# First block's compression: the blocks held stationary, both weight halves streamed in one matmul, the rows folded by a constant, and the logits behind map 0's scores

## The chip, the cores and the metric

The kernel runs on one core of one Trainium2 chip. What counts is the device time of the whole program, in microseconds (us), as the median of some runs. Three runs of the kernel before took 1732.04, 1733.45 and 1734.22 us. All arithmetic is in float32 (weights and activations of the large products are held as two fp32r parts).

## What is computed

A program of four layers on one sequence of 256 tokens with 1024 channels: two layers of the "first block" and two of the "second block". The change touches the first block alone, and in it the attention over compressed keys and values. Cut to that:

```python
def compress(t, pos_emb, w1, b1, w2):            # t: 256 tokens, 2 groups, 64 channels
    # 15 overlapping blocks of 32 tokens each, stride 16
    flat = blocks(t + pos_emb).reshape(15, 2, 32 * 64)
    hid = gelu(flat @ w1 + b1)                   # w1: 2048 x 128
    return hid @ w2                              # w2: 128 x 64
...
kc = compress(kcb, ..., cmp_w1[0], ...)          # n = 0 in the kernel: keys
vc = compress(vcb, ..., cmp_w1[1], ...)          # n = 1: values
s_c = einsum(q_raw, kc) * scale                  # 8 heads, 256 queries, 15 blocks
p_c = masked_softmax(s_c, ...)
o_b = gate0 * (p_c @ vc) + gate1 * (selected attention) + gate2 * (window attention)
```

## The kernel before

**Weights.** Every weight arrives in chunks of 1 MB in the ring `raw` (3 slots), issued by SyncE (`load`; the load of chunk c waits until chunk c - 3 is split). ScalarE rounds a chunk to its high part `whi` (two halves, L543), VectorE subtracts to get the low part `wlo` (L893); both have rings of 4 slots. `split_to(c)` does this, and where it stands in the queues of ScalarE and VectorE is written out by hand, mostly three chunks ahead of the products. A slot comes free when the sums that read it are done.

**Tiles.** `tile` makes 128 output channels for 256 tokens: for each of 8 pieces k of the contraction one matmul with `whi` as stationary operand and 512 columns (activations high | low, L1457) and one with `wlo` and 256 columns (L1460). Columns 0 to 255 and 256 to 511 of the bank are two parts of the sum: ScalarE copies the second to `low` (`low_copy`), VectorE adds the first (`tile_sum`, L901) and signals `tile_out`. Tile t uses bank t % 4, with exceptions in `EXTRA` and `PLACED`, and waits for the sum of tile t - 4.

**A layer of the first block.** Eight chunks of `w_in`, with rotary products between them; then the gate chunks `early 0` to `early 3`, each of two tiles. Beside the 16 steps of `early 0` run those of `compress(0)`, beside `early 1` those of `compress(1)`: after each pair of tile matmuls one with `whi` stationary and 60 columns (15 blocks x 2 groups, high | low, `RH`, L1608), one with `wlo` and 30 columns (L1609). The chunks are numbered through: `early 0` is chunk 8 of layer 0, the first compression chunk 9, `early 1` 10, the second compression chunk 11, `early 2` and `early 3` 12 and 13, then come the chunks of the branches, 14 and on. ScalarE and VectorE pass the same order as steps c of a loop; c = 9 and 11 are the compression's. There the 30 columns are summed into `HC`, and GELU is applied.

Then come, on TensorE: tile `early 2,0` (the first of the pair), a wait for both halves of `HC`, the second-stage products (L1678, L1680), tile `early 2,1`, a wait for ScalarE's copy to `KC` and `VC`, the logits (16 products of 64 rows, L1690), a wait for the sum of `early 2,1`, and the attention loop over 18 maps. Its steps i = 0 and 1 hold the scores of maps 0 and 1 (L1715), each followed by a tile of `early 3`; in steps 2 and 3 the compressed probabilities `PC` are transposed (L1726) and copied by ScalarE to `PCT` (shown as U). On VectorE the logits' mask, maximum and subtraction (L1107 to L1116) stand ahead of map 0; the sum of `early 2,1` stands behind the split of chunk 15 (`split_to(p["early"][3][0] + 2)`), on ScalarE too. Layer 1 is the same code.

## Time and profile before

| | |
|---|---|
| median of three runs | 1733.45 us |
| the profiled execution | 1734.53 us |
| its span, first to last instruction | 1732.7 us |
| granted TensorE clock, mean of the span | 0.998 of 2.4 GHz |
| TensorE busy (matmuls / weight loads) | 1705.6 us, 98% / 1455.9 us, 84% |
| VectorE, ScalarE, GpSimd busy | 1221.0 us, 70%; 1022.4 us, 59%; 690.5 us, 40% |
| compression products L1608, L1609 | 64 each, of 9926 matmuls in all |
| chain of work that ended last, by engine | PE 76%, DVE 17%, ACT 3% |

The busy share of TensorE counts a matmul from start to modelled end, and they overlap; how fast the queue moves is read from the starts of successive matmuls. PE is TensorE's matmuls, PEld its weight loads, DVE VectorE, ACT ScalarE, POOL GpSimd, SP SyncE.

### The profile page before, as it was taken

To read this page: it belongs to the slowest core of one execution; us is meant where nothing else is said; L and a number is where in the kernel's file an instruction comes from. 1 tells how busy PE (TensorE), PEld (TensorE's weight loads), DVE (VectorE), ACT (ScalarE), POOL (GpSimd) and SP (SyncE) were. 2 spreads that over 40 slices of the span, in tenths; PEclk is the share of its full clock that TensorE was granted. 3 is DMA by queue.
4 is the path that set the end of the run, shared out by engine and by line. 5 is a ranking of instruction groups with operands and counts; after the bars stand their busy time and mean duration, and the time that the engine had idled before them with its cause. 6 is when DMAs were issued, how large, how long until landed. Compare 5 with 4: busy or idle time off the path is not lost.

```text
span 1732.7 us, 26430 instructions
## 1 busy us (share of the span) xinstructions
PE 1705.6 (98%) x9926; PEld 1455.9 (84%) x9926; DVE 1221.0 (70%) x1840; ACT 1022.4 (59%) x1928; POOL 690.5 (40%) x666
## 2 busy tenths in 40 slices
PE   8999999999999999999999999999999999999998
PEld 7867898888867898889888888888898889788887
DVE  7776799957766799957666656766476656566663
ACT  5577666655577666646555556555465545565542
POOL 4135256701035256604661050765057600507640
PEclk9999999999999999999999999999999999999999
DMA  9633576576524576576766553866576565348662
GB/s 271 175 98 109 171 208 182 174 244 175 146 77 122 170 201 189 182 231 173 193 183 223 176 172 98 234 184 206 178 201 188 183 231 193 123 124 224 187 208 73
DMA packets 412226, 306.73 MB, mean 177 GB/s; under 512 B 10083, under 2 KB 366901, under 8 KB 412098
## 3 DMA queue, kind: packets, MB, share of 16 engines
q1 hardware_dynamic: 411314, 304.31, 59.8%
q8 instruction: 79, 1.29, 0.3%
q0 software_dynamic: 784, 0.72, 0.2%
q14 instruction: 49, 0.40, 0.1%
HBM read 303.94 MB, written 1.05 MB: 176 GB/s over the span
## 4 chain that ended last, share of the span: by engine, by line
PE 76%; DVE 17%; ACT 3%; issue 3%; DMA 1%; DVEq 0%; SPq 0%; ACTq 0%
PE bank L1457 26%; PE bank L1460 13%; PE bank L1557 8%; PE bank L1559 8%; PE bank L1558 8%; DVE wlo L893 6%; DVE CB L1221 6%; PE bank L1523 3%; PE bank L1520 3%; DVE UB L901 2%; PE bank L1491 1%; PE bank L1764 1%; ACT PB L546 1%; PE bank L1739 1%; PE bank L1715 1%
## 5 line engine op out<-in xcount | busy, mean ns | idle before, releaser
L893 DVE TENSOR_TENSOR wlo<-raw,whi 128x1024 fp32r<-128x1024 f32 (+1 forms) x568 | 735.9, 1319 | 174.2 <-ACT whi L543 170.6
L1457 PE MATMUL bank<-hsA,whi 128*128 128x512 f32 x2480 | 797.5, 398 | 0.0
L543 ACT ACTIVATE whi<-raw 128x1024 fp32r<-128x1024 f32 (+1 forms) x568 | 571.4, 1034 | 133.9 <-PE bank L1559 89.1
L1460 PEld LDWEIGHTS bank<-hsA,wlo 128*128 128x128 f32 x2480 | 467.1, 188 | 105.8
L1460 PE MATMUL bank<-hsA,wlo 128*128 128x256 f32 x2480 | 495.6, 279 | 0.0
L1457 PEld LDWEIGHTS bank<-hsA,whi 128*128 128x128 f32 x2480 | 384.6, 189 | 3.0 <-issue 2.2
L543 ACT ACTIVATE low<-bank 128x256 f32<-128x256 f32 (+1 forms) x404 | 150.3, 376 | 315.8 <-PE bank L1457 289.0
L1325 POOL TENSOR_TENSOR HB<-CB,UB 128x256 f32<-128x256 f32 x88 | 123.6, 1405 | 343.3 <-ACT CB L546 342.7
L1557 PE MATMUL bank<-whi,hid 128*128 128x512 f32 x528 | 206.1, 390 | 2.0 <-DVE wlo L893 2.0
L1559 PE MATMUL bank<-wlo,hid 128*128 128x512 f32 x528 | 205.5, 389 | 0.0
L1558 PE MATMUL bank<-whi,hid 128*128 128x512 f32 x528 | 205.4, 389 | 0.0
L901 DVE TENSOR_TENSOR UB<-bank,low 128x256 f32<-128x256 f32 x264 | 109.2, 416 | 113.0 <-ACT low L543 112.8
L1326 POOL TENSOR_TENSOR hid<-CB,UB 128x256 fp32r<-128x256 f32 x88 | 144.9, 1646 | 0.0
L1557 PEld LDWEIGHTS bank<-whi,hid 128*128 128x128 f32 x528 | 99.1, 188 | 23.0 <-DVE wlo L893 2.8
L1325 POOL TENSOR_TENSOR HB<-CB 128x256 f32<-128x256 f32 x44 | 62.0, 1408 | 139.5 <-ACT CB L546 139.5
L1559 PEld LDWEIGHTS bank<-wlo,hid 128*128 128x128 f32 x528 | 99.1, 188 | 20.6
L1558 PEld LDWEIGHTS bank<-whi,hid 128*128 128x128 f32 x528 | 99.1, 188 | 20.5
L1221 DVE SCALAR_TENSOR_TENSOR CB<-UB,convT,CB 128x256 f32<-128x256 f32 x176 | 114.0, 705 | 0.0
L1327 POOL TENSOR_TENSOR hid<-HB,hid 128x256 fp32r<-128x256 f32 x132 | 109.7, 831 | 10.4
L1523 PE MATMUL bank<-hsA,wlo 128*128 128x256 f32 x464 | 96.5, 284 | 0.0
L1520 PE MATMUL bank<-hsA,whi 128*128 128x256 f32 x464 | 94.2, 283 | 0.0
L1523 PEld LDWEIGHTS bank<-hsA,wlo 128*128 128x128 f32 x464 | 78.8, 192 | 0.7
(226 smaller groups left out, 1896.1 us busy)
## 6 DMA issues: line engine op xcount, KB each, us to landing
raw<-in_ffn_w_up SPq DMA_DIRECT2D x176, 512.0 KB, 5.3
raw<-in_ffn_w_down SPq DMA_DIRECT2D x120, 512.0 KB, 4.5
raw<-in_w_in SPq DMA_DIRECT2D x104, 512.0 KB, 5.9
raw<-in_ffn_w_gate SPq DMA_DIRECT2D x88, 512.0 KB, 4.1
raw<-in_w_out SPq DMA_DIRECT2D x32, 512.0 KB, 4.5
raw<-in_ffn_w_down SPq DMA_DIRECT2D x24, 256.0 KB, 2.9
G<-in_norm_g SPq DMA_DIRECT2D x12, 512.0 KB, 7.2
raw<-in_cmp_w SPq DMA_DIRECT2D x8, 512.0 KB, 5.4
```

What stands on the lines that cost most here:

```text
L543: return nc.scalar.activation(out_, in_, func, **kw)
L893: v.tensor_tensor(wlo[c_ % RING][:, x:y], raw[:, c_ % RAW, x:y], whi[c_ % RING][:, x:y].bitcast(F32), ALU.subtract)\
L1221: ins = v.scalar_tensor_tensor(y[:, n, :], UB[:, j % 2, n, k:S + k], convT[:, k, at:at + 1], y[:, n, :], ALU.mult, ALU.add)
L1325: g_.tensor_tensor(HB[:, j % 2, :], x, y, ALU.mult)
L1326: seq.link(g_.tensor_tensor(dst[:, 0:S], x, y, ALU.mult))
L1457: return mm(out_[:, 0:2 * n], whi[slot][:, at:at + P], rhs[:, 0:2 * n], start=x == 0, stop=False, **g32)
L1460: return mm(out_[:, n:2 * n], wlo[slot][:, at:at + P], rhs[:, 0:n], start=False, stop=False, **g32)
L1520: return mm(out_, whi[c % RING][:, at(m, k):at(m, k) + P], both(k, 1), start=False, stop=j == 0 and k == KD - 1, **g32)
L1523: return mm(tile_bank(t + m)[:, S:2 * S], wlo[c % RING][:, at(m, k):at(m, k) + P], hsA[:, k, 0:S], start=False, stop=j > 0 and k == KD - 1 ...
L1557: mm(y, hi, whi[s][:, x * HALF:x * HALF + HALF], start=k == k_first, stop=False, **g32)
L1558: mm(y, lo, whi[s][:, x * HALF:x * HALF + HALF], start=False, stop=False, **g32)
L1559: ins = mm(y, hi, wlo[s][:, x * HALF:x * HALF + HALF], start=False, stop=k == k_end, **g32)
```

## The change

- The compression's product is turned round. Stationary is now a window of 128 columns of the blocks (`RHP`: the 60 columns of step k, the 60 of step k + 1 and 8 more; behind the last step 68 columns of zeros), moving are 128 columns of `whi` and the same 128 of `wlo`, in one matmul of 256 columns. For that both lie in one tensor `whl`. The result has blocks in its rows (0 to 59 count) and hidden units in its columns.
- ScalarE copies the 60 x 128 of the second half, VectorE adds the first into `HE`. A new product per n, `fold`, multiplies `HE` with a constant 128 x 30 matrix: it adds rows i and i + 30 and transposes, into bank 7 or 6. GELU reads that bank. `fold(0)` stands behind the first tile of `early 1`, `fold(1)` behind `early 2,0`.
- `HE` and the zeros are filled by GpSimd at the start of each layer's rotation products, `KC` (now zero-padded by parity of the head) once by VectorE at the start.
- The second-stage products stand behind `early 2,1`. The logits are 8 products of 128 rows against the padded `KC`, 30 columns each, and stand behind the scores of map 0 on TensorE; on VectorE their part stands behind map 0, on ScalarE their exponential behind map 0's.
- The splits at c = 9 and 11 move behind the compression's copy and sum; the split of chunk 15 moves behind the sum of `early 2,1` on both engines, and on VectorE its second half behind the logits.

```diff
...
-    whi = [sb(f"whi{n}", [P, CH], F32R)[0] for n in range(RING)]
-    wlo = [sb(f"wlo{n}", [P, CH], F32R)[0] for n in range(RING)]
+    whl = sb("whl", [P, RING, 2, CH], F32R)[0]
+    whi, wlo = [[whl[:, n, x, :] for n in range(RING)] for x in range(2)]
...
+    HE = sb("HE", [P, 2, P], at=hsB_at + 4096)[0]
+    RHP, _, rh_end = sb("RHP", [P, 2, 16 * 4 * N_CMP + 68], F32R, at=hsB_at + 8128)
...
@@ scalar, steps c
-                if not early:
+                if not early and c not in (9, 11):
                     split_to(in_cs[c] + 3)
...
                 if c in (9, 11):
-                    low_copy(p["cmp"][c // 2 - 4][1], n=30)
+                    t = p["cmp"][c // 2 - 4][1]
+                    act.wait_ge(sum_ready, t + 1)
+                    f(low[0:4 * N_CMP, t % 4, 0:P], tile_bank(t)[0:4 * N_CMP, P:2 * P], ACT.Copy).then_inc(low_ready, 1)
...
                 if c in (9, 11):
+                    split_to(in_cs[c] + 3)
                     n = c // 2 - 4
-                    act.wait_ge(tile_out, p["cmp"][n][1] + 1)
-                    f(HC[:, n, :], HC[:, n, :], ACT.Gelu_apprx_tanh,
+                    act.wait_ge(cmp_fold, 2 * L + n + 1)
+                    f(HC[:, n, :], bank[7 - n][:, S:S + 2 * N_CMP], ACT.Gelu_apprx_tanh,
...
             low_copy(third)
+            low_copy(third + 1)
             act.wait_ge(cmp_kv, L + 1)
...
-            f(KC[:, :], bank[6][:, 0:30], ACT.Copy)
+            for e in range(2):
+                r = slice(HD * e, HD * e + HD)
+                f(KC[r, :, N_CMP * e:N_CMP * e + N_CMP], bank[6][r, 0:30].rearrange("p (g c) -> p g c", g=2), ACT.Copy)
             f(VC[0:N_CMP, :, :], ...).then_inc(cmp_kv_out, 1)
             split_to(p["early"][3][0] + 2)
-            low_copy(third + 1)
-            act.wait_ge(cmp_x, L + 1)
-            f(PC[:, :, :, 0:N_CMP], PC[:, :, :, 0:N_CMP], ACT.Exp, scale=SCALE).then_inc(cmp_e, 1)
...
+                if i == 0:
+                    act.wait_ge(cmp_x, L + 1)
+                    f(PC[:, :, :, 0:N_CMP], PC[:, :, :, 0:N_CMP], ACT.Exp, scale=SCALE).then_inc(cmp_e, 1)
@@ vector
-                    tile_sum(p["cmp"][c // 2 - 4][1], HC[:, c // 2 - 4, :], n=30)
+                    n, t = c // 2 - 4, p["cmp"][c // 2 - 4][1]
+                    dve.wait_ge(low_ready, t + 1)
+                    dve.wait_ge(cmp_clear, 2 * L + 2)
+                    r = slice(0, 4 * N_CMP)
+                    v.tensor_tensor(HE[r, n, :], tile_bank(t)[r, 0:P], low[r, t % 4, 0:P], ALU.add).then_inc(tile_out, 1)
+                    split_to(in_cs[c] + 3)
...
             tile_sum(third, gate_place(2)[:, 0, :])
-            split_to(p["early"][3][0] + 2)
             tile_sum(third + 1, gate_place(2)[:, 1, :])
+            split_to(p["early"][3][0] + 2, 0)
...
+                if i == 0:
+                    cmp_scores()
+                    split_to(p["early"][3][0] + 2)
@@ gpsimd
+            pool.wait_ge(ht_ready, h_at(2 * L, 1, 1))
+            g_.memset(HE[:, :, :], 0.0).then_inc(cmp_clear, 1)
+            g_.memset(RHP[:, :, 16 * 4 * N_CMP:].bitcast(F32), 0.0).then_inc(cmp_clear, 1)
@@ tensor
-                        mm(out_[:, 0:60], whi[slot][:, k * P:k * P + P], RH[:, n, k, :], start=k == 0, stop=False, **g32)
-                        ins = mm(out_[:, 30:60], wlo[slot][:, k * P:k * P + P], RH[:, n, k, 0:30], start=False, stop=k == 15, **g32)
+                        at = k * 4 * N_CMP
+                        ins = mm(out_[:, 0:2 * P].rearrange("p (x j) -> p x j", x=2), RHP[:, n, at:at + P],
+                                 whl[:, slot, :, k * P:k * P + P], start=k == 0, stop=k == 15, **g32)
...
+            def fold(n):
+                pe.wait_ge(tile_out, p["cmp"][n][1] + 1)
+                if n == 0:
+                    pe.wait_ge(swap_used, 11 * L + len(ROPE))
+                mm(bank[7 - n][:, S:S + 2 * N_CMP], HE[:, n, :], C("fold"), start=True, stop=True, **g32).then_inc(cmp_fold, 1)
...
             for m in range(2):
                 early_tile(1, m, compress(1)(m))
+                if m == 0:
+                    fold(0)
             early_tile(2, 0)
+            fold(1)
+            early_tile(2, 1)
             pe.wait_ge(cmp_hid, 2 * L + 2)
...
             ins.then_inc(cmp_kv, 1)
-            early_tile(2, 1)
-            pe.wait_ge(cmp_kv_out, L + 1)
...
+            def cmp_scores():
+                pe.wait_ge(cmp_kv_out, L + 1)
+                for qb in range(2):
+                    for j in range(4):
+                        at = (4 * qb + j) * 32
+                        ins = mm(bank[7][:, at:at + 2 * N_CMP], U1[:, QB + j, qb * P:qb * P + P], KC[:, j // 2, :],
+                                 start=True, stop=True, **g32)
+                ins.then_inc(cmp_z, 1)
...
-            pe.wait_ge(tile_out, third + 2)
+            pe.wait_ge(tile_out, max(t for t in range(third + 2) if t % 4 < 2) + 1)
...
                     if i == 1:
-                        pe.wait_ge(cmp_x, L + 1)
+                        pe.wait_ge(gates_ready, L + 1)
...
+                if i == 0:
+                    cmp_scores()
+                    pe.wait_ge(tile_out, third + 2)
```

## Rows read from the trace of the kernel before

**Rows 1.** TensorE's timeline, plain tiles: start us, us, engine, line, operation, count

```profile
62.13 0.63 PE L1457 MATMUL bank<-hsA,whi 128*128 128x512 f32 x2
...
62.83 0.62 PE L1457 MATMUL bank<-hsA,whi 128*128 128x512 f32 x2
```

**Rows 2.** TensorE's timeline beside the compression, layer 0, first to last of eight steps

```profile
74.35 0.19 PE L1608 MATMUL bank<-RH,whi 128*128 128x60 f32 x1
74.38 0.26 PE L1609 MATMUL bank<-RH,wlo 128*128 128x30 f32 x1
74.49 0.48 PE L1457 MATMUL bank<-hsA,whi 128*128 128x512 f32 x1
...
79.08 0.48 PE L1457 MATMUL bank<-hsA,whi 128*128 128x512 f32 x1
```

**Rows 3.** TensorE's timeline, first and last of 27 starts, 256 columns

```profile
24.84 0.28 PE L1520 MATMUL bank<-hsA,whi 128*128 128x256 f32 x1
...
27.96 0.28 PE L1520 MATMUL bank<-hsA,whi 128*128 128x256 f32 x1
```

**Rows 4.** TensorE's timeline, layer 0, second stage to transposes; [idle before <-releaser]

```profile
94.39 0.41 PE L1678 MATMUL bank<-HC,w2cur 128*128 128x30 f32 x2 [1.25 <-ACT HC L546]
...
95.05 0.50 PE L1457 MATMUL bank<-hsA,whi 128*128 128x512 f32 x1
...
98.04 1.96 PE L1690 MATMUL bank<-KC,U 64*128 64x15 f32 x32
...
100.47 0.50 PE L1457 MATMUL bank<-hsA,whi 128*128 128x512 f32 x1
...
107.74 1.05 PE L1726 MATMUL bank<-const,PC 128*15 128x128 f32 x8
```

**Rows 5.** VectorE's timeline, layer 0

```profile
90.26 0.75 DVE L901 TENSOR_TENSOR SGE<-bank,low 128x256 f32<-128x256 f32 x2
...
96.48 2.36 DVE L893 TENSOR_TENSOR wlo<-raw,whi 128x1024 fp32r<-128x1024 f32 x2 [1.42 <-ACT whi L543]
...
100.12 0.60 DVE L1107 TENSOR_TENSOR PC<-bank,const 128x60 f32<-128x60 f32 x4 [0.94 <-PE bank L1690]
...
101.73 0.35 DVE L1146 CUSTOM_DVE_ANT_0 PB<-bank,const,nsink 128x128 f32<-128x128 f32 x1
...
104.48 0.48 DVE L1146 CUSTOM_DVE_ANT_0 PB<-bank,const,nsink 128x256 f32<-128x256 f32 x1
```

**Rows 6.** ScalarE's timeline, layer 0

```profile
95.25 0.25 ACT L543 ACTIVATE VC<-bank 15x128 f32<-15x128 f32 x1
95.40 1.99 ACT L543 ACTIVATE whi<-raw 128x1024 fp32r<-128x1024 f32 x2
...
106.60 0.19 ACT L546 ACTIVATION_READ_ACCUMULATOR PB<-PB,st 128x1 f32 x1
...
108.39 1.06 ACT L543 ACTIVATE U<-bank 15x512 f32<-15x512 f32 x2 [0.79 <-PE bank L1726]
```

**Rows 7.** Chain of waits, layer 0: start us, us, what

```profile
28.61 0.86 PE bank L1657 x4
...
121.42 0.66 PE bank L1764 x8
```

**Rows 8.** Page, costliest groups: busy us, mean ns, idle before and releaser

```profile
L543 ACT ACTIVATE low<-bank 128x256 f32<-128x256 f32 (+1 forms) x404 | 150.3, 376 | 315.8 <-PE bank L1457 289.0
```

**Rows 9.** TensorE's timeline, layer 1

```profile
479.33 0.50 PE L1457 MATMUL bank<-hsA,whi 128*128 128x512 f32 x1
...
485.47 0.34 PE L1715 MATMUL bank<-U 64*128 64x128 f32 x1 [1.18 <-DVE SGE L901]
```

**Rows 10.** ScalarE's timeline, layer 1

```profile
495.56 1.06 ACT L543 ACTIVATE U<-bank 15x512 f32<-15x512 f32 x2 [0.79 <-PE bank L1726]
```

**Rows 11.** Chain of waits, layer 1

```profile
471.27 10.24 DMA raw<-in_w_in
```

**Rows 12.** Stretches, layer 1: busy us (count) of each engine, granted clock, DMA, GB/s

```profile
486.00:488.00 2.00, 2.00 (x10) 1.60 (x7) 1.93 (x11) 0.40 (x1) 0.00 (x0) 0.55 0.95 287
```

More of the change, by code:

```diff
@@ L43 @@
 CONST = {"ident": 128, "swap": 128, "ntri": 128, "stick": 128, "mask_a": 256, "mask_c": 256, "pair": 24,
-         "mask_cmp": 32, "count": 32, "width": 2, "freq": 1, "sign": 1}
+         "mask_cmp": 32, "count": 32, "width": 2, "freq": 1, "sign": 1, "fold": 2 * N_CMP}
 CONST_AT, _n = {}, 0
@@ L76, in host_constants @@
     put("sign", np.where(i % 64 < 32, -1.0, 1.0))
+    put("fold", (i[:, None] < 4 * N_CMP) & (i[:, None] % (2 * N_CMP) == np.arange(2 * N_CMP)[None, :]))
     return c
@@ L212, in build @@
     stc = sb("stc", [P, 4, 16])[0]
-    KC = sb("KC", [P, 30])[0]
+    KC = sb("KC", [P, 2, 2 * N_CMP])[0]
     VC = sb("VC", [16, 2, HD], at=cq_at)[0]
@@ L984, in _ @@
         v.memset(col[:, 1:2], 1.0)
+        v.memset(KC[:, :, :], 0.0)
         def turns():
@@ L1068, in _ @@
                 early = L == 0 and c < 4
-                if not early:
+                if not early and c not in (9, 11):
                     split_to(in_cs[c] + 3)
@@ L1113, in per_row @@
                 return stc[:, k, :].unsqueeze(2).broadcast_to([P, 16, N_CMP])
-            seq.link(v.tensor_reduce(stc[:, 0, :], rowsP, AX_X, ALU.max))
-            seq.link(v.tensor_scalar(stc[:, 0, :], stc[:, 0, :], 0.1 * NEG, None, ALU.max))
-            v.tensor_tensor(rowsP, rowsP, per_row(0), ALU.subtract).then_inc(cmp_x, 1)
+            def cmp_scores():
+                dve.wait_ge(gates_ready, L + 1)
+                dve.wait_ge(cmp_z, L + 1)
+                z = bank[7][:, 0:S].rearrange("p (b h c) -> p b h c", b=2, h=4)
+                mask = C("mask_cmp").rearrange("p (b c) -> p b c", b=2)
+                for qb in range(2):
+                    for par in range(2):
+                        ins = v.tensor_tensor(PC[:, qb, par:8:2, 0:N_CMP], z[:, qb, :, N_CMP * par:N_CMP * par + N_CMP],
+                                              mask[:, qb:qb + 1, 0:N_CMP].broadcast_to([P, 4, N_CMP]), ALU.add)
+                seq.link(ins)
+                seq.link(v.tensor_reduce(stc[:, 0, :], rowsP, AX_X, ALU.max))
+                seq.link(v.tensor_scalar(stc[:, 0, :], stc[:, 0, :], 0.1 * NEG, None, ALU.max))
+                v.tensor_tensor(rowsP, rowsP, per_row(0), ALU.subtract).then_inc(cmp_x, 1)
             gate = gates[:, :, :].rearrange("p b (h n) -> p (b h) n", n=3)
@@ L1682, in _, with cmp_scores @@
             ins.then_inc(cmp_kv, 1)
-            early_tile(2, 1)
-            pe.wait_ge(cmp_kv_out, L + 1)
-            pe.wait_ge(rope_done, 11 * L + len(ROPE))
-            for qb in range(2):
-                for h in range(8):
-                    r, at = HD * (h % 2), (4 * qb + h // 2) * 16
-                    ins = mm(bank[7 - 2 * (h % 2)][:, at:at + N_CMP], U1[r:r + HD, QB + h // 2, qb * P:qb * P + P],
-                             KC[r:r + HD, N_CMP * (h // 4):N_CMP * (h // 4) + N_CMP], start=True, stop=True, **g32)
-            ins.then_inc(cmp_z, 1)
-            third, fourth = p["early"][2][1], p["early"][3][1]
+            third, fourth = p["early"][2][1], p["early"][3][1]
+            def cmp_scores():
+                pe.wait_ge(cmp_kv_out, L + 1)
+                for qb in range(2):
+                    for j in range(4):
[3 more added lines that the diff above has]
+                ins.then_inc(cmp_z, 1)
+            pe.wait_ge(rope_done, 11 * L + len(ROPE))
             pe.wait_ge(kswap_done, 3 * L + 3)
-            pe.wait_ge(tile_out, third + 2)
+            pe.wait_ge(tile_out, max(t for t in range(third + 2) if t % 4 < 2) + 1)
             done = len(MAPS) * L
```

16 lines of the change are left out of this document (5 added, 11 removed).

## The prediction

> **What bounds the kernel now.** I read the page first: TensorE is busy 98% of the span (the table above), so time goes only where TensorE's queue gets shorter or where it stands still. Then TensorE's timeline in the stretch that the diff touches, once in each layer of the first block (about 71 to 108 us, and 455 to 496 us), then ScalarE and VectorE in the same stretch, and last the chain of waits behind it. Times of the first layer (layer 0) are in us from the span's start.
>
> Ahead of the stretch and behind it nothing is edited but small fills. What has to be found is by how much the attention loop is entered earlier in each layer. Everything behind is bounded by TensorE and its weights are prefetched only three chunks deep, so I take the shift as kept to the end of the program.
>
> **Compression products.** Two plain matmul pairs of a tile (512 and 256 columns each) repeat every 0.70 us, 0.35 a pair [rows 1]. With the compression beside them eight steps take 79.08 - 74.49 = 4.59 us, 0.575 a step [rows 2]. The 60-column and the 30-column matmul thus cost 0.225 us a step, though their columns are few: the 30-column one starts 0.03 us after the other, and the next tile matmul another 0.11 later [rows 2]. That is the pace of 128-column weight loads which nothing covers. The change puts one load and one 256-column matmul in the place of two and two. 256 columns cost 0.12 us where moving data comes in two pieces of 128 at stride, as it will here: 27.96 - 24.84 = 3.12 us from the first to the last of 27 starts, the load hidden [rows 3]. New step 0.35 + 0.12 = 0.47, saved 0.105. Bounds: 0.117 (the column pace of the plain tile, 0.35 x 256/768) and 0.23 (load exposed, 0.11 more). There are 32 steps in a layer: **-3.4 us** (bounds -3.5 and +0.2).
>
> By the Trainium skill (TensorE: Matmul & The Clock Gate, LDWEIGHTS and Back-to-back issue gap) a load takes as long as its number of columns, 128/1.2 = 107 ns, and 256 columns stream in 109 ns; an estimate from these would hide the load by 2 ns and give a step of 0.46, 0.3 us more saved in a layer. The rule also speaks against the change, since 60 of the 128 columns of a window would do: padded, the load has no slack left. The rows agree on the 0.11.
>
> **Folding.** Two new f32 products a layer, 128 columns stationary, 30 moving. The nearest rows are the f32 products of the second stage, which come as two instructions of 30 and four of 64 columns between 94.39 and 95.05, 0.11 each [rows 4]: 0.22 to 0.33 each fold, 0.3 taken, **+0.6 us**. The fold waits for VectorE's sum of the 60 rows. For `fold(1)` (layer 0): TensorE ends `early 2,0` at 94.39 - 1.25 = 93.1 today [rows 4], 3.4 - 0.3 earlier then, 90.0. VectorE begins the two sums of `early 1` at 90.26, right behind its split of chunk 13, and they take 0.75 [rows 5]; that split moves by 1.7 (below), so the sums end at 89.3 and `HE`, priced at 0.2, at 89.5. No wait, with 0.5 us in hand.
>
> **The hidden layer's wait.** Today TensorE stands still 1.25 us until GELU is done [rows 4], because the second-stage product sits in the middle of tile pair `early 2`. Moved behind the pair it has 2.8 us of cover (eight pairs): **-1.25 us**.
>
> **Logits.** 16 products of 64 rows become 8 of 128 rows. Every f32 product is two instructions; 32 of 64 rows now run in pairs, one on each half of the array, 1.96 us for the 32 [rows 4], so 0.11 a pair, and 16 full-height ones at 0.11 take the same 1.8 us. **0**; less instructions buy nothing (bounds -0.9 if each took half a pair, +0.1). The Trainium skill (TensorEngine Tiling, Theoretical Speedup) gives two row tiles up to twofold and so says that the change throws that away; the row agrees, and it is just as much as the halved count gives back. The gap before the logits, 98.04 - (95.05 + 2.8) = 0.2 us, goes, since map 0's scores now stand before them: `KC` is copied in two halves, one copy (0.1 us) more before `cmp_kv_out`.
>
> TensorE in layer 0: second stage done at 95.05 - 3.4 + 0.6 - 1.25 + 2.8 (tile 2,1 now ahead) = 93.8. Logits and map 0's scores take 98.04 to 100.47 today, 2.43 [rows 4]; done at 96.2. Tile `early 3,0` started at 100.47: **-4.3 us** there, and the transposes of the probabilities, today 107.74, at 103.45.
>
> **What is late next.** The chain runs on through ScalarE: from its copy of the transposed probabilities at 108.39 [rows 6] it is the chain's main engine until TensorE takes over at 121.4 [rows 7]. So the entry is that copy, and it has a second way of being late. VectorE and ScalarE in the new order: `cmp_kv_out` follows the second stage by 95.50 - 95.05 = 0.45 us, plus 0.1 [rows 4, 6]: 94.35. Then ScalarE splits the first half of chunk 15 (half of 1.99) to 95.35, VectorE its half (half of 2.36) to 96.5 [rows 5, 6], and both stand ahead of map 0 in their queues. VectorE then has map 0 and the normalising (101.73 to 104.48, 2.75), the logits (100.12 to 101.73, 1.61) and the second half of the split (1.18), in all to 102.05; map 1 and its exponentials (104.48 to 106.79) 104.35 [rows 5, 6]; one copy of a tile half, 0.38 [rows 8]: **104.75**, against 104.05 by TensorE. 108.39 - 104.75 = **-3.65 us in layer 0**.
>
> Layer 1 runs the same code 384.3 us later, by one instruction in both, the first of tile `early 2,1` (95.05 and 479.33) [rows 4, 9]. Its entry is at 495.56 today, 111.26 in layer-0 time, 2.9 later than there [rows 6, 10]. The chain shows why: the load of chunk 15 was 10.24 us under way, to 481.51 [rows 11]; ScalarE's split waited for it, VectorE behind that, the tile sum behind that, and TensorE lost 1.18 us [rows 9]. Then its clock fell to 0.55 of full, the 1.2 GHz level for most of 486 to 488 [rows 12]. The change takes the sum out from behind the split. But it leaves map 0 and the logits behind the split's first half. That load is issued after the split of chunk 12, which moves with the first 16 steps, 1.7 us; landing at 479.8, 95.5 in layer-0 time, where ScalarE could start at 94.35. So everything of the chain is 1.15 us later than in layer 0: entry 105.9, and 111.26 - 105.9 = **-5.35 us in layer 1**. In layer 1 map 0 must also wait for the sum of `early 2,1` (banks 0 and 1), 0.4 us; the 2 us of slack that TensorE has there hide it.
>
> **Small things.** GpSimd fills `HE` and the tail of `RHP` before its first rotation product: nearest rows 0.1 to 0.3 us each, and TensorE, behind it, has no idle time in its timeline from 24 to 48 us; 0. VectorE's fill of `KC` at the start lies before its wait for ScalarE; 0. SyncE: loads 15 to 17 come 1.7 to 2 us earlier, load 18 about 2 us later, for a chunk used only behind the attention loop; 0. `RH` padding moves no bytes.
>
> **Sum.** -3.65 - 5.35 = -9.0 us. On the profiled execution 1734.5 - 9.0 = 1725.5; that execution is 1.1 us above the median, so the median becomes 1733.45 - 9.0 = **1724.4 us**.
>
> **The rivals.** (a) *Chunk 15 lands in time in layer 1*: its slow load may be an accident of what else is in flight, and in layer 0 the same load holds nobody up. Then layer 1 gains 6.5: **1723.3 us**. (b) *The load of the window is not hidden* (0.11 more a step): for it, that load and stream are within 0.01 us of each other. The second stage ends 3.4 us later again, entry 108.1 in both layers, -0.3 and -3.2: **1729.9 us**. (c) *The fold becomes the wait*: `HE` is summed behind a chunk split and two tile sums, in hand are 0.5 us. Beyond that it is paid in full in layer 0, and in layer 1 less the 1.15 us that chunk 15 hides. Late by 2.1 us, 1.6 beyond: 1.6 + 0.45 = 2.05, **1726.4 us**. (d) *Clock*: three microseconds of small products in a row (to 96.2) are new, and at the level of 1.2 GHz the tiles behind them would cost 1.5 us more; TensorE has 0.7 us in hand in layer 0 and 2 in layer 1, so 0.8 us: **1725.2**, within the forecast. The Trainium skill (TensorE: Matmul & The Clock Gate, HAM oscillation) has idle gaps as the cause; such a gap precedes the fall of [rows 9, 12], and the change removes it. (e) *The other side*: the 256-column matmul runs at the pace of unsplit f32, 0.86 us for four, twice over (0.43) [rows 7], if one operand is not taken as fp32r. That adds 0.31 a step, 19.8 us in all: **1744 us**. It decides from 0.26 us per matmul on. Against it: all three operands are declared fp32r.
>
> **How the numbers follow.** Forecast with (d) 0.62; (a) 0.14; (b) 0.08; (c) 0.10; (e) 0.04; other 0.02. Range: (a) with fold and step at their lower bounds, 1721.0; up to between (c) and (b), 1729.0. A difference of 0.2% (3.5 us) is about what a measurement of this kernel can tell from none: (b) lies on that line. Faster 0.88, same 0.07, slower 0.05.
>
> **What would show it.** Steps with compression at 0.47 us; fold 0.3 us with no idle before it; no idle before the second stage; logits still 1.8 us; tile `early 3,0` at 96.2; ScalarE's copy of the probabilities at 104.75 in layer 0 and at 495.56 - 9.0 = 486.6 in layer 1 (all there is shifted by layer 0's gain); the wait of ScalarE for chunk 15 still there in layer 1; the fall of the clock behind it gone. Wrong would be: a step of 0.58, or an attention loop that starts earlier but leaves ScalarE later than 121.4 - 3.65, or a shift that shrinks in a later stage.

## The result, and the profile after

| | before | after |
|---|---|---|
| median | 1733.84 us (1732.04 to 1734.43, 4 runs) | 1724.54 us (1723.51 to 1726.55, 4 runs) |
| the profiled execution | 1734.53 us | 1723.51 us |
| its span | 1732.7 us | 1721.7 us |
| granted TensorE clock, mean | 0.998 | 1.000 |
| matmuls | 9926 | 9838 |

The ratio is 0.995, 95% interval 0.9939 to 0.9962: 9.3 us less, where 9.0 had been forecast. Run again later in two more series, the changed kernel took 1724.29 and 1724.85 us.

The page of the changed kernel, busy times and share of the span; the shares are those of before within a point:

```profile
span 1721.7 us, 26269 instructions
PE 1697.1 (99%) x9838; PEld 1448.0 (84%) x9838; DVE 1220.8 (71%) x1841; ACT 1023.1 (59%) x1930; POOL 691.8 (40%) x670
```

Times of two executions can't be laid side by side as they stand: the first compression product is at 71.38 us before and at 70.72 us after, with nothing edited ahead of it but fills. So I count layer 0 from that product, layer 1 from layer 0's entry, and the rest from layer 1's entry. "Entry" is ScalarE's copy of the transposed probabilities, as in the prediction.

| | before | after | difference | forecast |
|---|---|---|---|---|
| first compression product | 71.38 | 70.72 | -0.66 | 0 |
| layer 0: to the entry | 37.01 | 32.94 | -4.07 | -3.65 |
| entry to entry | 387.17 | 380.89 | -6.28 | -5.35 |
| entry of layer 1 to the end of the span | 1237.1 | 1237.15 | 0 | 0 |

TensorE's timeline in layer 0 (columns as in [rows 1]; answers to [rows 2, 4]). L1482 and L1485 are the tile's two matmuls, L1635 the compression, L1647 the fold, L1716 and L1718 the second stage, L1754 map scores, L1729 the logits, L1768 the transposes:

```profile
79.29 0.39 PE L1482 MATMUL bank<-hsA,whl 128*128 128x512 f32 x1
79.52 0.28 PE L1635 MATMUL bank<-whl,RHP 128*128 128x256 f32 x1
...
80.22 0.39 PE L1482 MATMUL bank<-hsA,whl 128*128 128x512 f32 x1
...
82.10 0.39 PE L1482 MATMUL bank<-hsA,whl 128*128 128x512 f32 x1
...
82.44 0.30 PE L1647 MATMUL bank<-const,HE 128*128 128x30 f32 x2
82.58 0.48 PE L1482 MATMUL bank<-hsA,whl 128*128 128x512 f32 x1
...
83.25 0.39 PE L1482 MATMUL bank<-hsA,whl 128*128 128x512 f32 x1
...
88.98 0.40 PE L1482 MATMUL bank<-hsA,whl 128*128 128x512 f32 x1
89.21 0.30 PE L1647 MATMUL bank<-const,HE 128*128 128x30 f32 x2
89.35 0.47 PE L1482 MATMUL bank<-hsA,whl 128*128 128x512 f32 x1
...
92.23 0.30 PE L1716 MATMUL bank<-HC,w2cur 128*128 128x30 f32 x2
...
92.79 0.37 PE L1754 MATMUL bank<-U 64*128 64x128 f32 x1
...
93.62 1.97 PE L1729 MATMUL bank<-KC,U 128*128 128x30 f32 x16
95.43 0.48 PE L1482 MATMUL bank<-hsA,whl 128*128 128x512 f32 x1
...
102.67 1.05 PE L1768 MATMUL bank<-const,PC 128*15 128x128 f32 x8
```

What to see: two steps in 80.22 - 79.29 = 0.93 us; no idle time at either fold, and the two steps around the first take 83.25 - 82.10 = 1.15 us, 0.22 more than two steps elsewhere; no idle time before the second stage, where 1.25 us stood in [rows 4]; 1.81 us from the logits to the tile behind them, as before.

ScalarE's timeline in layer 0 (answers to [rows 6]) and VectorE's (answers to [rows 5]):

```profile
93.30 0.27 ACT L548 ACTIVATE VC<-bank 15x128 f32<-15x128 f32 x1
93.47 1.99 ACT L548 ACTIVATE whl<-raw 128x1024 fp32r<-128x1024 f32 x2
...
102.30 0.20 ACT L551 ACTIVATE st<-st 128x2 f32<-128x2 f32 x1 [2.90 <-DVE st L1170]
...
103.66 1.05 ACT L548 ACTIVATE U<-bank 15x512 f32<-15x512 f32 x2
```

```profile
88.53 0.27 DVE L1098 TENSOR_TENSOR HE<-bank,low 60x128 f32<-60x128 f32 x1
...
94.55 1.23 DVE L904 TENSOR_TENSOR whl<-raw,whl 128x1024 fp32r<-128x1024 f32 x1 [1.28 <-ACT whl L548]
...
98.58 1.22 DVE L904 TENSOR_TENSOR whl<-raw,whl 128x1024 fp32r<-128x1024 f32 x1
...
101.18 0.48 DVE L1165 CUSTOM_DVE_ANT_0 PB<-bank,const,nsink 128x256 f32<-128x256 f32 x1
```

The entry follows ScalarE's exponentials of map 1 without idle time, and these waited 2.90 us for VectorE: VectorE's queue, with both halves of the split in it, sets the entry, as forecast, not the transposes.

Layer 1, TensorE, ScalarE, chain of waits, and a stretch (busy us and count of PE, PEld, DVE, ACT, POOL, then granted clock, DMA share, GB/s), answering to [rows 9 to 12]:

```profile
472.46 0.30 PE L1716 MATMUL bank<-HC,w2cur 128*128 128x30 f32 x2
...
473.65 0.34 PE L1754 MATMUL bank<-U 64*128 64x128 f32 x1 [0.56 <-DVE SGE L912]
```

```profile
474.34 2.00 ACT L548 ACTIVATE whl<-raw 128x1024 fp32r<-128x1024 f32 x2 [0.54 <-DMA raw<-in_w_in]
...
484.55 1.05 ACT L548 ACTIVATE U<-bank 15x512 f32<-15x512 f32 x2
```

```profile
465.12 9.20 DMA raw<-in_w_in
```

```profile
476.00:478.00 2.00, 2.00 (x14) 1.78 (x14) 1.97 (x12) 1.66 (x3) 0.00 (x0) 1.00 1.19 295
```

The load of chunk 15 is still waited for, but only 0.54 us, and the clock is full, where [rows 12] had 0.55.

### The profile page after: what moved, and what is told of

It reads as the page before. It is cut to its first block, busy times and chain, and to the rows that moved or that the text cites. A ratio compares the mean times of both kernels' runs of the same rounds, so it can differ in the third digit from the quotient of the medians.

```text
span 1721.7 us, 26269 instructions
## 1 busy us (share of the span) xinstructions
PE 1697.1 (99%) x9838; PEld 1448.0 (84%) x9838; DVE 1220.8 (71%) x1841; ACT 1023.1 (59%) x1930; POOL 691.8 (40%) x670
## 4 chain that ended last, share of the span: by engine, by line
PE 75%; DVE 17%; ACT 3%; issue 3%; DMA 1%; DVEq 0%; SPq 0%; ACTq 0%
PE bank L1482 26%; PE bank L1485 13%; PE bank L1582 8%; PE bank L1583 8%; PE bank L1584 8%; DVE whl L904 6%; DVE CB L1243 6%; PE bank L1548 3%; PE bank L1545 3%; DVE UB L912 2%; PE bank L1516 1%; ACT PB L551 1%; PE bank L1806 1%; PE bank L1781 1%; DVE hsA L976 1%
## 5 line engine op out<-in xcount | busy, mean ns | idle before, releaser
L904 DVE TENSOR_TENSOR whl<-raw,whl 128x1024 fp32r<-128x1024 f32 (+1 forms) x568 | 735.5, 1318 | 169.4 <-ACT whl L548 165.8
L1482 PE MATMUL bank<-hsA,whl 128*128 128x512 f32 x2480 | 793.4, 397 | 0.0
L548 ACT ACTIVATE whl<-raw 128x1024 fp32r<-128x1024 f32 (+1 forms) x568 | 571.3, 1034 | 141.2 <-PE bank L1584 85.9
L1485 PEld LDWEIGHTS bank<-hsA,whl 128*128 128x128 f32 x2480 | 466.0, 188 | 105.5
L1485 PE MATMUL bank<-hsA,whl 128*128 128x256 f32 x2480 | 491.9, 278 | 0.0
L1482 PEld LDWEIGHTS bank<-hsA,whl 128*128 128x128 f32 x2480 | 384.0, 189 | 3.9 <-issue 2.4
L1582 PE MATMUL bank<-whl,hid 128*128 128x512 f32 x528 | 206.1, 390 | 2.0 <-DVE whl L904 2.0
L1584 PE MATMUL bank<-whl,hid 128*128 128x512 f32 x528 | 205.5, 389 | 0.0
L1583 PE MATMUL bank<-whl,hid 128*128 128x512 f32 x528 | 205.4, 389 | 0.0
L1582 PEld LDWEIGHTS bank<-whl,hid 128*128 128x128 f32 x528 | 99.1, 188 | 23.1 <-DVE whl L904 2.9
L1584 PEld LDWEIGHTS bank<-whl,hid 128*128 128x128 f32 x528 | 99.1, 188 | 20.7
L1583 PEld LDWEIGHTS bank<-whl,hid 128*128 128x128 f32 x528 | 99.1, 188 | 20.4
L1349 POOL TENSOR_TENSOR hid<-HB,hid 128x256 fp32r<-128x256 f32 x132 | 109.6, 831 | 10.3
L1548 PE MATMUL bank<-hsA,whl 128*128 128x256 f32 x464 | 96.4, 284 | 0.0
L1545 PE MATMUL bank<-hsA,whl 128*128 128x256 f32 x464 | 94.2, 283 | 0.0
L1548 PEld LDWEIGHTS bank<-hsA,whl 128*128 128x128 f32 x464 | 78.8, 191 | 0.7
```

The lines of the kernel that those rows point to most:

```text
L548: return nc.scalar.activation(out_, in_, func, **kw)
L904: v.tensor_tensor(wlo[c_ % RING][:, x:y], raw[:, c_ % RAW, x:y], whi[c_ % RING][:, x:y].bitcast(F32), ALU.subtract)\
L1482: return mm(out_[:, 0:2 * n], whi[slot][:, at:at + P], rhs[:, 0:2 * n], start=x == 0, stop=False, **g32)
L1485: return mm(out_[:, n:2 * n], wlo[slot][:, at:at + P], rhs[:, 0:n], start=False, stop=False, **g32)
L1545: return mm(out_, whi[c % RING][:, at(m, k):at(m, k) + P], both(k, 1), start=False, stop=j == 0 and k == KD - 1, **g32)
L1548: return mm(tile_bank(t + m)[:, S:2 * S], wlo[c % RING][:, at(m, k):at(m, k) + P], hsA[:, k, 0:S], start=False, stop=j > 0 and k == KD - 1 ...
```

## The experiments

All comparisons with the kernel before are between runs of one chip. Where an experiment's share of the gain is given for a layer, it is taken from its profiled execution with the three marks of the table above.

### One half alone: the turned product and the fold

The order of second stage, logits and splits of chunk 15 is that of before; the product, the fold, the padded `KC` and the moved splits at c = 9 and 11 stay.

```diff
@@ scalar
-            low_copy(third + 1)
@@ ... behind split_to(p["early"][3][0] + 2)
+            low_copy(third + 1)
+            act.wait_ge(cmp_x, L + 1)
+            f(PC[:, :, :, 0:N_CMP], PC[:, :, :, 0:N_CMP], ACT.Exp, scale=SCALE).then_inc(cmp_e, 1)
@@ vector: the split of 15 ahead of tile_sum(third + 1), cmp_scores() behind it
@@ tensor
             fold(1)
-            early_tile(2, 1)
             pe.wait_ge(cmp_hid, 2 * L + 2)
...
+            early_tile(2, 1)
...
+            cmp_scores()
```

> The changed kernel with the turned product and the folds kept, but the order of before for the rest: second stage in the middle of tile pair early 2 (behind fold(1)), logits ahead of map 0, sum of early 2,1 behind the split of chunk 15. Theory (TensorE's queue to the second stage, then the landing of chunk 15 in layer 1): 32 steps of 0.467 in place of 0.575, -3.5 us, folds at 0.14 each, +0.3; the wait for GELU about 0.5 us in place of 1.25. Layer 0 enters the attention loop 4.0 us earlier than before; in layer 1 the start of map 0 hangs on the landing of chunk 15, which moves by only 1.7 us, so only that is gained there and the stall of TensorE before map 0 grows from 1.2 to over 3 us, with the fall of the clock behind it. In all -5.7 us, 1728.1. Rival (the gain is simply a sum of TensorE's terms): -4.0 in both layers, 1725.8, stall unchanged.

Measured: 1728.57 us (1727.23 to 1729.81), ratio 0.9971 (0.996 to 0.9982). Layer 0 -3.91, entry to entry -2.53. TensorE's timeline in layer 0, then in layer 1, then two stretches of layer 1 in the columns used above:

```profile
90.03 0.41 PE L1712 MATMUL bank<-HC,w2cur 128*128 128x30 f32 x2 [0.38 <-ACT HC L551]
```

```profile
478.49 0.43 PE L1752 MATMUL bank<-U 64*128 64x128 f32 x1 [2.68 <-DVE SGE L911]
```

```profile
478.00:480.00 2.00, 1.51 (x9) 1.29 (x10) 1.90 (x10) 0.22 (x1) 0.00 (x0) 0.67 0.77 186
480.00:482.00 2.00, 2.00 (x8) 1.71 (x8) 1.90 (x13) 1.06 (x5) 0.00 (x0) 0.50 1.08 377
```

The wait for the hidden layer has fallen from 1.25 to 0.38 us with the old order: GELU now follows the fold directly, and VectorE sums ahead of its split. In layer 1 the opposite: the earlier the compression is done, the longer the sum of `early 2,1` waits behind chunk 15. ScalarE waits 2.83 us for the load, TensorE 2.68 us for the sum (1.18 in [rows 9]), and the clock falls to its lower level. The product saves 3.9 us in layer 0 and 2.5 in layer 1: some 1.4 us of it is taken back there, less than the 2.3 that had been expected.

### The other half alone: the order

The product of before (two matmuls a step, `whi` and `wlo` stationary), no fold; everything in the new order.

```diff
-                        ins = mm(out_[:, 0:2 * P].rearrange("p (x j) -> p x j", x=2), RHP[:, n, at:at + P],
-                                 whl[:, slot, :, k * P:k * P + P], start=k == 0, stop=k == 15, **g32)
+                        mm(out_[:, 0:60], whi[slot][:, k * P:k * P + P], RH[:, n, k, :], start=k == 0, stop=False, **g32)
+                        ins = mm(out_[:, 30:60], wlo[slot][:, k * P:k * P + P], RH[:, n, k, 0:30], start=False, stop=k == 15, **g32)
...
-                if m == 0:
-                    fold(0)
...
-            fold(1)
```

> The changed kernel with the product of before (two matmuls of 60 and 30 columns a step, the sum of 30 columns into HC, no fold), all else of the change kept. Theory: steps at 0.575 again; second stage without a wait. The entry of the attention loop (ScalarE's copy of the transposed probabilities) follows cmp_kv_out by the same 10.2 us as in the changed kernel: layer 0 about 1.1 us earlier than before (107.3). Layer 1: no stall ahead of map 0 but 0.5, no fall of the clock, entry 3.9 earlier than before in addition. In all -5.0 us, 1728.8. Rival (most of layer 1's gain comes from the shorter products): -1.1 in layer 0 and as much in layer 1, 1731.6, with stall and slow clock still there.

Measured: 1730.5 us (1729.11 to 1731.75), ratio 0.998 (0.9972 to 0.9989). Layer 0 -1.32, entry to entry -4.14. ScalarE doesn't wait for chunk 15 and the clock is 1.00 in layer 1 from 474 us on; TensorE waits for the sum of `early 2,1` as forecast, 0.56 us:

```profile
480.29 0.34 PE L1749 MATMUL bank<-U 64*128 64x128 f32 x1 [0.56 <-DVE SGE L912]
```

The two local gains, -1.32 - 4.14 = -5.46, lie within 0.5 us of what was expected; the median moved by 3.3 only (more on this in the part on the sum and the median). The halves together: -3.91 - 1.32 in layer 0 against -4.07 of the whole, since both take from the same wait for the hidden layer (0.87 of its 1.25 us goes by the first half alone) and the whole is held by VectorE; -2.53 - 4.14 = -6.67 against -6.28 from entry to entry.

### Only the sum ahead of the split, in the kernel before

```diff
@@ scalar
-            split_to(p["early"][3][0] + 2)
             low_copy(third + 1)
+            split_to(p["early"][3][0] + 2)
@@ vector
-            split_to(p["early"][3][0] + 2)
             tile_sum(third + 1, gate_place(2)[:, 1, :])
+            split_to(p["early"][3][0] + 2)
```

> The kernel before with one thing moved: copy and sum of tile early 2,1 ahead of the split of chunk 15, on ScalarE and VectorE. Theory: layer 0 unchanged. In layer 1 TensorE's wait of 1.18 us ahead of map 0 and the slow clock behind it (1.5 us) go; the logits' mask and maximum on VectorE are still behind the split, 0.3 us of the loss stays. -2.5 us, 1731.3. Rival (the chain through the split is the limit, the sum's place does not matter): the entry stays at 495.6, 1733.8; or the clock falls all the same: -1.2, 1732.6.

Measured: 1731.88 us (1731.12 to 1733.3), ratio 0.9992 (0.9983 to 1.0001). Layer 0 +0.18, entry to entry 384.45, which is -2.72. No stall of TensorE for that sum and a clock of 1.00 throughout layer 1. Before, layer 1's entry lay 387.17 - 384.3 = 2.9 us further behind layer 0's than the same instruction's distance [rows 4, 9] would have it; this edit of four lines takes 2.7 of them. So in the traced execution the late entry of layer 1 was that sum behind chunk 15, and the clock behind it. The median moved by 1.9 us with an interval that touches no change.

### The kernel before, once more

> The kernel before once more, for its profile. Theory: the late landing of chunk 15 in layer 1, TensorE's wait of over 1 us ahead of map 0 and the slow clock behind it are there in every execution; distance from the entry of layer 0 to that of layer 1 387.2 us as in the first profile. Rival: they differ from execution to execution (distance between 384.3 and 387.2), and the median contains only part of them.

Measured: 1734.15 us. The stall and the clock return, by TensorE's timeline, ScalarE's, the chain and a stretch:

```profile
485.01 0.34 PE L1715 MATMUL bank<-U 64*128 64x128 f32 x1 [1.09 <-DVE SGE L901]
```

```profile
481.08 2.00 ACT L543 ACTIVATE whi<-raw 128x1024 fp32r<-128x1024 f32 x2 [1.66 <-DMA raw<-in_w_in]
```

```profile
470.90 10.16 DMA raw<-in_w_in
```

```profile
486.00:488.00 2.00, 2.00 (x8) 1.71 (x8) 1.93 (x12) 0.63 (x3) 0.00 (x0) 0.50 0.99 347
```

Entry to entry is 387.03 here and 387.17 there: neither stall nor fall is an accident of the first trace. That every execution has them does not follow from two traces, and the clocks of the others speak against it (see the part on the sum and the median).

### The changed kernel, twice more

> The changed kernel once more, timed beside the others on the same chip. Both theories: 1724.5 us, 9.3 below before; the entry of the attention loop 4.1 us earlier in layer 0 once the start of the program is taken off, ScalarE's wait for chunk 15 in layer 1 between 0 and 2 us.

Measured: 1724.29 us (1723.47 to 1726.03), ratio 0.9946 (0.9934 to 0.9958). Layer 0's entry is at 32.93, entry to entry takes 381.02, the wait for chunk 15 is 0.65 us, and the clock doesn't fall in either layer.

> The changed kernel itself, on the same chip as the 64-row logits. 1724.4 us by both theories; clock 1.00 in 96 to 102 us by theory A, by theory B it may as well fall here.

Measured: 1724.85 us (1724.13 to 1726.66), ratio 0.9952 (0.9935 to 0.9969). Here the two distances are 32.93 and 380.95, the wait is 0.58 us, and the clock is 1.00 in both layers. The distances repeat to 0.15 us in three executions; what varies is the place of the first compression product, 70.72, 71.56 and 71.91 us, ahead of all that was changed.

### Sixty columns of the window for 128

```diff
-                        ins = mm(out_[:, 0:2 * P].rearrange("p (x j) -> p x j", x=2), RHP[:, n, at:at + P],
+                        ins = mm(out_[0:4 * N_CMP, 0:2 * P].rearrange("p (x j) -> p x j", x=2), RHP[:, n, at:at + 4 * N_CMP],
```

> The changed kernel with the window cut to the 60 columns that count: 60 stationary columns in place of 128, result in rows 0 to 59 alone. Theory (in the changed kernel the load is hidden and the step is bound by its 1024 streamed columns): step stays 0.467 us, no change, 1724.4. Rival (the load of 128 columns is the last to end, the rule that a load takes as long as its columns): up to 0.01 us a step, 0.6 us in all, hardly to be seen; or a narrow load is slower, as the 15-column loads in the trace do not show: then the step grows above 0.5 and the time above 1726.

Measured: 1724.65 us (1723.34 to 1725.62), ratio 0.9944 (0.9932 to 0.9956). The next start is 0.12 us behind the product as before (72.87 to 72.99 in its timeline):

```profile
72.87 0.28 PE L1635 MATMUL bank<-whl,RHP 128*60 128x256 f32 x1
72.99 0.40 PE L1482 MATMUL bank<-hsA,whl 128*128 128x512 f32 x1
```

So the 128-column load is hidden behind the 256 columns, and rival (b) is out. In this execution the clock fell to 0.50 in layer 1 from 478 to 480 us, and entry to entry took 0.8 us more than in the changed kernel. Ahead of the fall stand the wait for the sum of `early 2,1`, 0.56 us as in the changed kernel, and the logits in their 128-row form. It was one execution; whether the narrower window has a part in it is open.

### The logits as 16 products of 64 rows

```diff
-                    for j in range(4):
-                        at = (4 * qb + j) * 32
-                        ins = mm(bank[7][:, at:at + 2 * N_CMP], U1[:, QB + j, qb * P:qb * P + P], KC[:, j // 2, :],
+                    for h in range(8):
+                        r, at = HD * (h % 2), (4 * qb + h // 2) * 32
+                        ins = mm(bank[7 - h % 2][:, at:at + N_CMP], U1[r:r + HD, QB + h // 2, qb * P:qb * P + P],
+                                 KC[r:r + HD, h // 4, N_CMP * (h % 2):N_CMP * (h % 2) + N_CMP], start=True, stop=True, **g32)
```

> The changed kernel with the logits as 16 products of 64 rows again, into two banks, in their new place. Theory (pairs of 64-row instructions run side by side, so halving their count bought nothing): the 32 instructions take 1.8 us as the 16 do; no change, 1724.4. Rival (each instruction has its own price of 0.11 us): 3.6 us, and since VectorE's chain hangs on them, up to 1.8 us more in a layer, 1728.

Measured: 1725.42 us (1725.05 to 1725.94), ratio 0.9948 (0.9935 to 0.996). The product itself is as short as forecast, 1.89 us to the next tile against 1.81. But layer 0's entry came 34.18 us behind the first compression product, not 32.94. TensorE's timeline and three stretches of layer 0:

```profile
94.51 1.86 PEld L1729 LDWEIGHTS bank<-KC,U 64*128 64x128 f32 x32 [0.31 <-ACT VC L548]
94.51 1.96 PE L1729 MATMUL bank<-KC,U 64*128 64x15 f32 x32
96.40 0.50 PE L1482 MATMUL bank<-hsA,whl 128*128 128x512 f32 x1
...
97.69 1.06 PE L1482 MATMUL bank<-hsA,whl 128*128 128x512 f32 x2
```

```profile
96.00:98.00 2.00, 2.00 (x18) 1.84 (x17) 1.97 (x12) 1.66 (x3) 0.00 (x0) 0.91 1.07 276
98.00:100.00 2.00, 2.00 (x7) 1.62 (x7) 1.90 (x8) 2.00 (x10) 0.00 (x0) 0.50 0.10 31
100.00:102.00 2.00, 2.00 (x11) 1.19 (x10) 1.86 (x6) 0.40 (x2) 0.00 (x0) 0.74 0.05 14
```

The clock is at its lower level (0.50 of full, 1.2 GHz) from 97.6 to 101.0 us by the shares of these stretches, and two tile matmuls take 1.06 us instead of 0.63. TensorE had waited 0.31 us for `VC` ahead of the logits, and not otherwise; from the last start of map 0's scores to the first of the logits it is 0.39 us here and 0.40 in the changed kernel, so this wait doesn't tell the two apart. In layer 1 ScalarE waited 1.19 us for chunk 15 in this execution, and entry to entry took 381.58 us. This was a result that no theory had named, so the kernel was run again beside the changed one:

> The changed kernel with the logits as 16 products of 64 rows again, run once more. In its first execution TensorE's granted clock fell to 0.50 in layer 0 behind the logits, where it had been 1.00 in both executions of the changed kernel, and the entry of the attention loop came 1.2 us later. Theory A: the lower clock belongs to the 64-row form standing behind map 0's scores, which are 64-row products too; then it is below 1.00 in layer 0 (96 to 102 us) again and the median is 1 us above that of the changed kernel run beside it (about 1725.4 against 1724.4). Theory B: it was an accident of one execution; then the clock is 1.00 there, layer 0's entry is 32.9 us behind the first compression product as in the changed kernel, and the medians agree within 0.5 us.

Measured: 1725.51 us (1723.59 to 1726.5), ratio 0.9952 (0.9937 to 0.9966). Its stretches in layer 0:

```profile
96.00:98.00 2.00, 2.00 (x10) 1.79 (x9) 1.97 (x14) 1.67 (x4) 0.00 (x0) 0.70 0.68 197
98.00:100.00 2.00, 2.00 (x8) 1.63 (x7) 1.90 (x5) 1.61 (x9) 0.00 (x0) 0.50 0.00 1
```

The fall repeats, with the entry at 34.24 us. In the three traced executions of the changed kernel the clock is 1.00 in these stretches and the entry at 32.93 or 32.94, and the four other traces with 128-row logits in this place (the order alone, sixty columns, chunk 15 twice) have no fall in layer 0 either. So theory A holds for the place and the cost, 1.3 us of layer 0. The medians differ by 0.7 us in one series and by 0.9 across two, in the expected sense, but within their spread. Over the whole span none of the nine executions with 64-row logits has a mean clock of 1.000, of the 13 of the changed kernel five have. Before the change the same 64-row products stood ahead of map 0's scores [rows 4] and brought no fall (clock 1.00 from 94 to 106 us), and in layer 1 they ran at full clock in both executions. Why the form and the place together bring the fall, and only in layer 0, is not settled; that a fall can follow the 128-row form too shows in layer 1 of the experiment with sixty columns.

### Chunk 15's split moved into the attention loop

ScalarE splits it in step 1 of the loop, VectorE one half each in steps 2 and 3, which takes the split out of the way of the entry.

```diff
@@ scalar
-            split_to(p["early"][3][0] + 2)
...
+                    if i == 1:
+                        split_to(p["early"][3][0] + 2)
@@ vector
-            split_to(p["early"][3][0] + 2, 0)
...
-                    split_to(p["early"][3][0] + 2)
...
+                if i in (2, 3):
+                    split_to(p["early"][3][0] + 2, i - 2)
```

> The changed kernel with the split of chunk 15 moved out from ahead of map 0: on ScalarE behind the first copy of early 3 (where it idles 2.9 us), on VectorE its halves at the end of steps 2 and 3 of the attention loop. Theory (after the change VectorE's chain through that split is late next): the entry is then set by TensorE's transposes, 0.4 us earlier in layer 0 and 0.6 to 1 in layer 1, where the landing of chunk 15 no longer matters: -1 us to -1.5 us, 1723.2. Rival (the split only moves to where ScalarE and VectorE are busier): what is won at the entry is lost in steps 2 to 6, no change; or, if VectorE becomes late with the maxima, +1.

Measured: 1726.21 us (1724.93 to 1727.61), ratio 0.9952 (0.9939 to 0.9966). The entry is 0.36 us earlier in layer 0 (32.58) and now waits for TensorE alone; from layer 1's entry to the end it is 1238.6 us, 1.5 more. ScalarE's timeline, then TensorE's:

```profile
104.47 1.06 ACT L548 ACTIVATE U<-bank 15x512 f32<-15x512 f32 x2 [0.79 <-PE bank L1769]
...
108.08 0.21 ACT L551 ACTIVATE st<-st 128x4 f32<-128x4 f32 x1 [0.51 <-DVE st L1170]
...
110.47 0.20 ACT L551 ACTIVATE st<-st 128x2 f32<-128x2 f32 x1 [0.17 <-DVE st L1170]
```

```profile
110.36 0.65 PE L1807 MATMUL bank<-PT,V 128*64 128x256 f32 x4 [0.97 <-ACT PT L548]
```

VectorE's two halves of 1.2 us (at 105.23 and 108.23 us) delay the maxima of later maps, and ScalarE stands still 0.51 + 0.17 us for them. The chain runs through VectorE's second half until 110.47 us, and then through ScalarE until about 118. The time moved out of the entry came back: entry to entry took 381.32 us, 0.43 more than in the changed kernel, so nothing was won at layer 1's entry, where 0.6 to 1 us had been expected, and 1.5 us were lost behind it. This place for the split doesn't beat the changed kernel; no other was tried.

### Chunk 15 of layer 1 from layer 0's weights

The load is issued at the same point, in the same pieces and to the same slot, but reads the same gate chunk of layer 0. One gate chunk of layer 1 thus has other weights.

```diff
-                    gate(L, x, c)
+                    gate(0 if x == 4 else L, x, c)
```

> The changed kernel, but chunk 15 of layer 1 is read from layer 0's weights (so one gate chunk of layer 1 has the wrong weights; all else is the same). If the late landing in layer 1 belongs to the place of the weights in memory, the load takes about as long as in layer 0 and ScalarE doesn't wait for it: entry of layer 1 at 380.3 us behind layer 0's instead of 380.9. If it belongs to what else is in flight, the load takes 9 to 10 us again and ScalarE waits 0.5 to 0.7 us.

Measured: 1723.3 us in one execution, span 1721.5. The two DMA issues of chunk 15 in layer 1 (count, KB each, median us to landing), in the changed kernel and in the experiment, and ScalarE's split of it in the experiment:

```profile
raw<-in_w_in SPq DMA_DIRECT2D x2, 512.0 KB, 7.3
```

```profile
raw<-in_w_in SPq DMA_DIRECT2D x2, 512.0 KB, 5.8
```

```profile
474.24 1.99 ACT L548 ACTIVATE whl<-raw 128x1024 fp32r<-128x1024 f32 x2
```

ScalarE doesn't wait: the load is 1.5 us shorter, about what chunk 15 takes in layer 0 of the changed kernel (5.7). Entry to entry is 380.25 us, and the distance of one instruction on TensorE between the layers, the second stage's first, is 472.46 - 92.23 = 380.23 us in the changed kernel: what layer 1's entry had lost, 0.66 us, was chunk 15 and nothing else. The late landing belongs to which weights are read, not to what else is in flight, for nothing else is altered. Whether it is their place in memory, or that layer 0's had been read once before, this one execution doesn't part.

## Why the prediction was right, and where by luck

**The compression product: right.** The last matmul of `early 2,0` starts at 92.74 us before, on TensorE's timeline:

```profile
92.74 0.40 PE L1457 MATMUL bank<-hsA,whi 128*128 128x512 f32 x1
```

That is 92.74 - 71.38 = 21.36 us behind the first compression product, and 88.98 - 70.72 = 18.26 us after, with one fold of 0.22 in it: 3.3 us saved by 32 steps, forecast 3.4. The price of [rows 3] for 256 columns at stride held, and so did the cover of the load.

**The fold: right in place, at the lower end in size.** 0.22 us each (1.15 - 0.93), the lower bound of 0.22 to 0.33, where 0.3 was taken. The tile matmul behind a fold starts 0.14 us after it, but the one behind that comes another 0.08 or 0.09 late (82.58 to 82.90 us, against 0.23 where no fold stands ahead), so the 0.11 for each f32 instruction, read from the second stage [rows 4], held. The 0.14 of the first experiment's expectation counts only the first of the two delays. `HE` was done at 88.80 and needed at 89.21: 0.4 us in hand, forecast 0.5. Rival (c) was as near as it looked, and didn't come.

**The hidden layer's wait: right** (no idle at 92.23). The first experiment adds that 0.87 us of the 1.25 would have gone by the earlier GELU alone.

**The logits: right on TensorE (1.81 us), and the reason for the change was missed.** "Less instructions buy nothing" holds for the queue. The 64-row form in the new place costs 1.3 us of layer 0 through the clock. My rival (d) had the clock fall behind "three microseconds of small products"; in layer 0 it didn't with 128-row products in seven traces, and it did with 64-row ones in two.

**TensorE's start of `early 3,0`:** 100.47 - 71.38 = 29.09 before, 95.43 - 70.72 = 24.71 after: -4.38, forecast -4.3, with small errors that cancel. The two folds are 0.16 us cheaper than taken and the second stage 0.1 (0.56 against 0.66), and from start to start the removed wait was worth some 0.2 more than its 1.25. Against that, a gap of 0.2 us before the logits, which I had let go, is still there (`VC` is copied until 93.57, the logits start at 93.62).

**The entry: right cause, 0.43 us too late in size.** Forecast 104.75 - 71.38 = 33.37 us behind the first compression product, measured 32.94. Map 1 begins on VectorE at 30.46 against 30.67, and from there to the entry 2.48 us against 2.70. Both are sums of durations read with their overlaps in.

**Layer 1: right cause, chunk 15 over-priced.** I had it 1.15 us late; it was 0.66. Its load was 9.20 to 9.32 us under way in three executions of the changed kernel against 10.24 and 10.16 before, and I had kept the 10.24 [rows 11]. With the 0.43 above this is nearly all of -6.28 against -5.35. The wait of map 0 for the sum was 0.56 against 0.4, and hidden, as said. Rival (a) didn't come: the slow load is no accident of one execution, it repeats, and goes with layer 1's weights. It cost about half of the 1.15 us, so that the local sum (-10.35) lies near (a)'s (-10.15) without (a)'s cause.

**The rest of the program: right.** From layer 1's entry to the end it is 1237.1 us in both profiled executions, and 1236.8 to 1237.3 in the other three of the two kernels.

**The sum and the median.** Local gains add up to -10.35 us, 1.35 more than the sum of -9.0, while the median fell by 9.3. The spans of the profiled executions, 1732.7 and 1732.4 before, 1721.7, 1722.5 and 1722.6 after, differ by 10.3 on average, so the local reading is sound; the medians of the other executions differ by 0.8 to 1.0 us less. For the order alone the same gap is 2 us (5.46 against 3.3), for the sum alone 0.7 (2.54 against 1.9).

The granted clock recorded for every execution tells where a good part of it comes from. The kernel before was timed 39 times beside the experiments. In both of its traces the stretch from 485 to 490 us has a clock of 0.66; that alone takes 0.34 x 5 = 1.7 us of full clock, 0.001 of the span, off the mean. Yet 11 of the 39 have a mean of 1.000, which leaves no room for it. Beside the first experiments these were 8 of 23, 1732.0 us on average, against 1734.5 for the other 15. The sum ahead of the split averages 1732.0 in 11 executions, all at 0.999 or 1.000. That is 2.5 us below the 15, its local gain, and nothing below the 8. So the stall and the fall seem to be in about two executions of three, and the median holds them only in part: the rival put down ahead of the second trace of the kernel before is borne out that far, by times and mean clocks, not by traces. The order alone has the reverse: its traced execution has 0.999, but six of its 11 have 0.998 and take 1.4 us more than the other five. Against the 15 the changed kernel (1724.5 on average in that series) gains 10.0 us, close to the local 10.35; the rest is open.

The predicted 1724.4 against 1724.54 is therefore closer than its parts, and by luck: two terms were too small by 1.35 us in all, and they had been read from an execution with the fall and taken off a median that holds it only in part, which shows 1 us less than the profile.

**Conclusions on the change.** By the medians of each half the turned product and fold bring 5.2 us and the order 3.3; by the local sums 6.4 and 5.5. In layer 1 the product alone makes the wait for chunk 15 worse, and only the order lets all of its gain through.

## What to carry to other kernels

Where stationary loads of 128 columns are followed by few moving columns, turn the product round: here 2 loads and 90 columns at 0.225 us became 1 load and 256 columns at 0.12. Before pricing such an edit, follow each engine's queue to the next instruction that waits for a DMA: whatever is made earlier runs into it, and a sum that others wait for must not stand behind it. And read local distances between fixed marks besides the median, since the start of the program alone moved by more than 1 us between executions.

## What the hardware showed that was not expected

- TensorE's clock fell to its lower level with no idle time over 0.31 us ahead of it, behind 32 instructions of 64 rows and 15 columns (0.50 of full in 98 to 100 us in both executions), and not behind 16 instructions of 128 rows and 30 columns in the same place and the same 1.8 us (1.00 in seven traces). In layer 1 it did fall once behind those 128-row instructions (0.50 in 478 to 480 us, sixty columns), with a wait of 0.56 us ahead that brought no fall in the three traces of the changed kernel. In the kernel before and in the first experiment the fall came behind a stall of 1.1 to 2.7 us.
- The Trainium skill (TensorE: Matmul & The Clock Gate, HAM oscillation) has idle gaps as what brings the fall. The trace of the kernel before agrees in kind, with gaps of 1.09 and 1.18 us that are shorter than the waits which the section describes; the 64-row logits do not fit, with nothing over 0.31 us ahead of the fall.
- Halves of 512 KB, issued at the same point, landed in 7.3 us from layer 1's weights and in 5.8 from layer 0's (one execution of the experiment; 7.3 in two of the changed kernel, 7.9 in the kernel before).
- Two f32 instructions of 30 columns on a 128-column stationary operand cost 0.22 us between tile matmuls: 0.14 to the next start, the rest at the one behind it. The six instructions of the second stage took 0.56 together (92.23 to 92.79).
- 60 or 128 stationary columns make no difference to the pace beside 256 moving ones (0.12 us).
